# Two blocks on one core: the second block's q, k, v and u weights split earlier, the pooling operand split between rounds of the top-k choice

## The chip, the cores and the metric

The kernel runs on one NeuronCore of a Trainium2 chip. The metric is the device time of one execution in microseconds (us). The kernel is one program in which five engines work side by side, each on its own list of instructions in program order: TensorE (PE), VectorE (DVE), ScalarE (ACT), GpSimd (POOL) and SyncE (SP), which issues the loads. They wait for each other through semaphores only.

## What is computed

256 rows of 1024 channels go through two blocks, all in float32. The change lies in the first half of the second block:

```python
h = rmsnorm_2(x, mix_norm[l])
z = h @ w_in[l]                      # 1024 -> 2632 columns
u = z[..., OFF_POOL:OFF_Q]           # 512, for the pooling mixer
q, k, v = ...                        # 512 columns each, 8 heads of 64
qi, ki, wi = ...                     # index queries 8 x 64, index key 64, index weights 8
q = apply_rope(rmsnorm_2(q, q_norm[l]), cos_a, sin_a)
k = apply_rope(rmsnorm_2(k, k_norm[l]), cos_a, sin_a)
qi = apply_rope(qi, cos_i, sin_i)
ki = apply_rope(rmsnorm_2(ki, idx_k_norm[l])...)
y_pool = pool_mixer(u, pool_w[l], pool_scale[l])      # windowed means, then 4 products of 128 x 128
y_attn = dsa_attention(q, k, v, qi, ki, wi)           # each row attends to its 64 best places
x = x + concat([y_pool, y_attn]) @ w_out[l]
# then memory cross-attention (wq, wo) and a mixture of 32 experts, 2 per row
```

`dsa_attention` scores all places with the index heads (the sum over heads of `relu(qi . ki) * wi`), keeps the 64 best per row, and runs a softmax over them.

## The kernel before

**Exact products.** A float32 weight is split into a high half and a low half of a format that TensorE multiplies fast. ACT writes the high half (`HI`, line 667), DVE writes the low half, weight minus high half (`ring_low`, line 1182), and for the eight names in `POOLED` POOL writes the low half (line 637). The left operand is split likewise into `AH` and `AL`. A product is then three matmuls (lines 1918 to 1920).

**Units.** `split_order()` lists the weights in the order of use; each is cut into units of 1024 columns per partition, which are numbered over all weights in `S`. In the part that matters the order is qi (4 units), kw (index key and weights, 1 unit), q (4), k (4), v (4), u (4), pool0, pool1, attn0, attn1 (2 each), wq, wo. On ACT `hi_to(n)` makes all high halves up to unit n, on DVE `lo_to(n)` all low halves up to n, passing over those of POOL. `HI` has 8 places, so the high half of unit n waits until TensorE is done with unit n - 8 (`s_un`). So the place where `hi_to` and `lo_to` stand in the lists of ACT and DVE says how far the splits run ahead of TensorE, and what stands in front of them.

**TensorE's order.** Strip qi, transposes of x, kw; strip q (after its third unit the memory keys are turned, `s_hdp`); strip k; the index queries and the index key are turned (`turn_heads`, `s_thp` 1 to 3); index scores (`pair_scores`, `s_scp`, line 2369); strip v; strip u, which waits for ACT's scaled copy of k (`s_z` 8); the pooling products (line 2390, `s_plp` 1 and 2); turning of q and k (`s_thp` 4 to 7); the four products with `pool_w` (line 2402, `s_plp` 3 and 4); the attention scores (`head_scores`, line 2412), which wait for all copies of q and k to `QT` and `KT` (`s_th` 8); then strips of the output projection (`strip_half`) between the steps of the softmax: `probabilities` turns exponentials (line 2421), `values` multiplies with v (line 2430), `rows_turned` turns the result (line 2437). A strip has twelve matmuls of 512 columns per unit; a `strip_half` works for one of the two row tiles and has six.

**ACT around it.** `z_out` copies a strip's result from PSUM to `Z`; `head_sums` sums the squares of 16 heads (line 681) and takes the roots (line 958); `heads_out` copies the strip scaled per head (line 966); line 978 is the root for the index key, line 998 the relu of the index scores. All of these and all `hi_to` stand in one list.

**DVE around it.** `head_sums` (index key: line 1492), `head_turned`, `head_cosine`, `head_sum` are the rotary steps (lines 1501, 1508, 1514), `head_recip` the reciprocal of the roots, `index_heads` the weighted sum over index heads, `index_round` one of 8 rounds of the choice of places (each takes the 8 largest per row, lines 1585 and 1589), `index_mask` the mask from them, `low_out` the low half of the pooling result (`AL`, line 1198).

**POOL** begins its 8 units of pool and attn when DVE has finished the rotary step of k (`s_hk` 8).

**SP** issues the loads in the order of use into a ring of 8 buffers, later 21, each load when its buffer's last user is done. The 96 expert weights of 1 MB each fill the ring from 515 us on.

## Time and profile before

| | us |
|---|---|
| median of 3 runs | 808.61 |
| lowest, highest | 799.5, 809.78 |
| profiled execution | 811.39 |
| its span, first to last instruction | 809.4 |
| TensorE busy | 726.8 (90%) |
| VectorE busy | 364.0 (45%) |
| ScalarE busy | 326.7 (40%) |
| GpSimd busy | 60.7 (8%) |

A profile is one execution on the chip. Times in it count from the first instruction. The stretch of the second block that the change touches lies between 426 and 523 us. PEclk is the clock that TensorE was granted, as a share of 2.4 GHz. A row of the timeline has the start, the duration, the engine, the line, the operation with what it writes and reads, how many instructions are merged, and in brackets the idle time before it with what ended it. Matmuls overlap, so that their durations are longer than the distance of their starts.

### The profile page before, as it was taken

How to read it: one execution, taken by the hardware profiler on the slowest of the kernel's cores; microseconds unless marked ns; L12 is line 12 of the kernel's file. 1: busy time of each engine (PE TensorE's matmuls, PEld its weight loads, DVE VectorE, ACT ScalarE, POOL GpSimd, SP SyncE). 2: the span in 40 equal slices, each digit the busy share in tenths (PEclk: the TensorE clock that was granted, in tenths of full speed). 3: DMA queues.
4: the chain of work that ended last, by engine and by line, in shares of the span. 5: the costliest groups of instructions: out<-in, count | busy, mean ns of one | idle time of the engine just before them, and what ended most of it. 6: DMA issues, size and time to landing. Idle time of an engine off the chain costs nothing.

```text
span 809.4 us, 13077 instructions
## 1 busy us (share of the span) xinstructions
PE 726.8 (90%) x5415; PEld 572.2 (71%) x5416; DVE 364.0 (45%) x745; ACT 326.7 (40%) x696; POOL 60.7 (8%) x71
## 2 busy tenths in 40 slices
PE   6697999989999999999999778997989999779785
PEld 4275677877999999999988556886775666345252
DVE  1453998456644566445586576443441111011011
ACT  2234465454533453334474894667331111001001
POOL 5000002000000002000000018072000000000000
PEclk8699899989999999999898999999979999989889
DMA  9997777616777754454463335455789999999994
GB/s 326 399 360 303 269 259 246 235 53 233 247 252 242 248 184 156 158 183 150 153 206 118 104 107 172 145 207 208 278 346 410 419 421 420 420 421 421 419 406 141
DMA packets 71475, 211.44 MB, mean 261 GB/s; under 512 B 7351, under 2 KB 34133, under 8 KB 55542
## 3 DMA queue, kind: packets, MB, share of 16 engines
q1 hardware_dynamic: 70370, 209.91, 69.0%
q0 software_dynamic: 800, 0.63, 0.4%
q8 instruction: 44, 0.72, 0.4%
q14 instruction: 17, 0.14, 0.1%
q10 hardware_dynamic: 244, 0.03, 0.0%
HBM read 209.51 MB, written 1.05 MB: 260 GB/s over the span
## 4 chain that ended last, share of the span: by engine, by line
PE 64%; DMA 11%; DVE 8%; ACT 6%; SPq 5%; issue 4%; ACTq 0%
PE ps L1918 10%; PE ps L1919 9%; PE ps L1920 9%; SPq L431 5%; PE ps L1931 5%; PE ps L1932 4%; PE ps L1933 4%; PE ps L2588 4%; DMA ring<-in_expert_w_up_dram 4%; DMA ring<-in_expert_w_gate_dram 3%; DVE ring_low L1182 3%; DMA ring<-in_ada_w_dram 2%; PE ps L2000 2%; PE ps L2564 2%; PE ps L2638 2%
## 5 line engine op out<-in xcount | busy, mean ns | idle before, releaser
L1182 DVE TENSOR_TENSOR ring_low<-ring,HI 128x1024 fp32r<-128x1024 f32 (+1 forms) x119 | 143.7, 1249 | 57.8 <-ACT HI L667 57.8
L667 ACT ACTIVATE HI<-ring 128x1024 fp32r<-128x1024 f32 (+1 forms) x135 | 133.9, 1056 | 46.9 <-DMA ring<-in_w_in_dram 45.8
L1918 PE MATMUL ps<-AH,HI 128*128 128x256 f32 x320 | 90.1, 282 | 0.3 <-DVE Z L1428 0.3
L1920 PE MATMUL ps<-AH,ring_low 128*128 128x256 f32 x320 | 89.6, 280 | 0.0
L1919 PE MATMUL ps<-AL,HI 128*128 128x256 f32 x320 | 89.4, 280 | 0.0
L1918 PE MATMUL ps<-HI,AH 128*128 128x512 f32 (+1 forms) x176 | 74.0, 421 | 12.1 <-DVE ring_low L1182 10.1
L2588 PE MATMUL ps<-ring,ZM 128*32 128x256 f32 x880 | 70.0, 413 | 15.3 <-DMA ring<-in_expert_w_up_dram 12.4
L1919 PE MATMUL ps<-ring_low,AH 128*128 128x512 f32 (+1 forms) x176 | 70.5, 401 | 0.0
L1920 PE MATMUL ps<-HI,AL 128*128 128x512 f32 (+1 forms) x176 | 69.7, 396 | 0.0
L2588 PEld LDWEIGHTS ps<-ring,ZM 128*32 128x32 f32 x880 | 38.1, 118 | 39.1 <-DMA ring<-in_expert_w_up_dram 15.8
L1918 PEld LDWEIGHTS ps<-AH,HI 128*128 128x128 f32 x320 | 60.1, 188 | 3.1 <-issue 2.5
L1931 PE MATMUL ps<-AH,HI 128*128 128x256 f32 x192 | 57.9, 302 | 3.3 <-DVE AL L1251 1.7
L1919 PEld LDWEIGHTS ps<-AL,HI 128*128 128x128 f32 x320 | 60.2, 188 | 0.0
L1920 PEld LDWEIGHTS ps<-AH,ring_low 128*128 128x128 f32 x320 | 60.1, 188 | 0.0
L1932 PE MATMUL ps<-AL,HI 128*128 128x256 f32 x192 | 55.3, 288 | 0.0
L1933 PE MATMUL ps<-AH,ring_low 128*128 128x256 f32 x192 | 55.0, 286 | 0.0
L637 POOL TENSOR_TENSOR ring_low<-ring,HI 128x1024 fp32r<-128x1024 f32 x16 | 39.7, 2520 | 196.8 <-DVE Z L1514 165.8
L1918 PEld LDWEIGHTS ps<-HI,AH 128*128 128x128 f32 x176 | 35.5, 201 | 26.5 <-DVE ring_low L1182 14.4
L1931 PE MATMUL ps<-AT,HI 128*128 128x256 f32 x176 | 49.3, 280 | 0.0
L1932 PE MATMUL ps<-AT,HI 128*128 128x256 f32 x176 | 49.2, 280 | 0.0
L1933 PE MATMUL ps<-AT,ring_low 128*128 128x256 f32 x176 | 49.2, 279 | 0.0
L1149 ACT ACTIVATE Z<-ps,GS 128x256 f32<-128x256 f32 x8 | 3.8, 474 | 110.2 <-issue 90.8
(382 smaller groups left out, 1310.9 us busy)
## 6 DMA issues: line engine op xcount, KB each, us to landing
ring<-in_expert_w_up_dram SPq DMA_DIRECT2D x28, 1024.0 KB, 25.3
ring<-in_expert_w_gate_dram SPq DMA_DIRECT2D x27, 1024.0 KB, 26.3
ring<-in_ada_w_dram SPq DMA_DIRECT2D x24, 1024.0 KB, 8.4
ring<-in_expert_w_down_dram SPq DMA_DIRECT2D x23, 1024.0 KB, 21.4
ring<-in_w_ffn_in_dram SPq DMA_DIRECT2D x20, 1024.0 KB, 6.2
ring<-in_w_in_dram SPq DMA_DIRECT2D x17, 1024.0 KB, 5.8
ring<-in_w_ffn_out_dram SPq DMA_DIRECT2D x11, 1024.0 KB, 7.3
ring<-in_w_out_dram SPq DMA_DIRECT2D x8, 1024.0 KB, 5.0
```

Source lines behind the costliest of these rows:

```text
L431: sp.dma_start(dst(views[s]), src, allow_slow_non_contiguous=True).then_inc(W.sems[s], 16)
L637: po.tensor_tensor(W.low(name)[:, o:o + w], W.view(name)[:, o:o + w], HI[:, u % UNITS, 0:w].bitcast(F32), ALU.subtract).then_inc(s_lp, 1)
L667: act(HI[:, i % UNITS, 0:w], W.view(name)[:, o:o + w], ACT.Copy).then_inc(s_hi, 1)
L1182: tt(W.low(name)[:, o:o + w], W.view(name)[:, o:o + w], HI[:, i % UNITS, 0:w].bitcast(F32), ALU.subtract).then_inc(s_lo, 1)
L1918: mm(dst, lh, rh, start=start, stop=False)
L1919: mm(dst, lh, rl, start=False, stop=False)
L1920: return mm(dst, ll, rh, start=False, stop=stop)
L1931: mm(dst, lh, rh, start=start, stop=False, skip_group_check=True)
L1932: mm(dst, lh, rl, start=False, stop=False, skip_group_check=True)
L1933: return mm(dst, ll, rh, start=False, stop=stop, skip_group_check=True)
L2000: ins = mm(ps[7 if q < 3 else 3][32 * j:32 * j + 32, :], cr[:, k, :], v[:, 512 * j:512 * j + 512], start=(k == 0), stop=(k == 7))
L2588: ins = mm(ps[UPB][CAP * j:CAP * j + CAP, 256 * h:256 * h + 256], XG[:, k, CAP * j:CAP * j + CAP], W.view(name)[:, 256 * k:256 * k + 256], ...
```

## The change

Nothing is added to or removed from the computation; instructions move in the lists of ACT, DVE and TensorE. On ACT the squares of the index key stand before the splits of k, and the splits of k, v and u each stand one strip further ahead: the high halves of v are made around the scaled copy of q, those of u around the scaled copy of k. On DVE the splits move likewise; the sum of the index key stands before the last split of q; the weighted sum over all index heads is in one piece before the rotary step of k; all rounds of the choice stand behind the last split of u; and the two halves of the pooling operand (`low_out`) stand behind rounds 6 and 7 instead of after all. On TensorE the turning of k comes after the products with `pool_w`, the copies to `KT` on ACT with it, and two half strips of pool0 and pool1 stand one step earlier in the softmax.

```diff
--- before.py
+++ after.py
@@ -940,7 +940,13 @@
                 else:
                     ac.wait_ge(s_un, S.end["kw"])
                 act(Z[:, t, 2560:NZ], ps[(1, 3)[t]][:, 0:NZ - 2560], ACT.Copy, scale=rs[:, t:t + 1]).then_inc(s_z, 1)
-            hi_to(S.first["q0"] + 3)
+            for t in range(NT):
+                ac.wait_ge(s_z, 2 + t + 1)
+                act(scq[t][:, 0:64], Z[:, t, 2560:2624], ACT.Square).then_inc(s_ha, 1)
+            hi_to(S.first["k0"])
+            ac.wait_ge(s_hki, 3)
+            act(st[:, 0:2], st[:, 0:2], ACT.Sqrt).then_inc(s_ha, 1)
+            hi_to(S.first["k0"] + 2)
 
             def head_sums(name, t0, banks, c0, c):
 
@@ -969,19 +975,11 @@
 
             ac.wait_ge(s_hdp, 1)
             act(KM[:, 0:2, :], ps[6][:, :].rearrange("p (h n) -> p h n", h=2), ACT.Copy, scale=C1[:, XQK + 1:XQK + 2]).then_inc(s_hda, 1)
-            hi_to(S.first["q0"] + 4)
-            hi_to(S.first["q0"] + 5)
-            for t in range(NT):
-                ac.wait_ge(s_z, 2 + t + 1)
-                act(scq[t][:, 0:64], Z[:, t, 2560:2624], ACT.Square).then_inc(s_ha, 1)
-            ac.wait_ge(s_hki, 3)
-            act(st[:, 0:2], st[:, 0:2], ACT.Sqrt).then_inc(s_ha, 1)
-            hi_to(S.first["q0"] + 6)
+            hi_to(S.first["k0"] + 3)
             head_sums("q1", "q", (4, 5), 16, 0)
-            hi_to(S.first["k0"] + 3)
+            hi_to(S.first["v0"])
             heads_out((4, 5), 16, 512, 1)
-            for i in range(1, 4):
-                hi_to(S.first["k0"] + i + 3)
+            hi_to(S.first["v0"] + 3)
 
             for pp in range(2):
                 ac.wait_ge(s_thp, pp + 1)
@@ -998,29 +996,31 @@
                         act(RR[t][:, 4 * quad + par:4 * quad + par + 3:2, 0:w],
                             ps[b][:, :].rearrange("p (i n) -> p i n", i=2)[:, :, 0:w], ACT.Relu).then_inc(s_rel, 1)
             head_sums("k1", "k", (0, 1), 32, 16)
-            hi_to(S.first["v0"] + 3)
+            hi_to(S.first["u0"])
             heads_out((0, 1), 32, 1024, 2)
-            for i in range(1, 4):
-                hi_to(S.first["v0"] + i + 3)
+            hi_to(S.first["u0"] + 3)
             z_out("v1", 1536, 512, (2, 3), "v")
-            for i in range(7):
-                hi_to(S.first["u0"] + i + 3)
+            hi_to(S.first["u0"] + 9)
             z_out("u1", 0, 512, (0, 1), "u")
             hi_to(S.first["wq0"] - 1)
 
             for h in range(2):
                 ac.wait_ge(s_plp, h + 1)
                 act(MT[:, 2 * h:2 * h + 2, :], ps[h][:, :].rearrange("p (g n) -> p g n", g=2), ACT.Copy).then_inc(s_pl, 1)
-            for i in range(4):
-                ac.wait_ge(s_thp, 4 + i)
-                dst, pp = (QT, KT)[i // 2], i % 2
-                act(dst[:, 2 * pp:2 * pp + 2, :], ps[4 + i][:, :].rearrange("p (h n) -> p h n", h=2), ACT.Copy).then_inc(s_th, 1)
+
+            def heads_copied(dst, i):
+                for pp in range(2):
+                    ac.wait_ge(s_thp, 4 + 2 * i + pp)
+                    act(dst[:, 2 * pp:2 * pp + 2, :], ps[4 + 2 * i + pp][:, :].rearrange("p (h n) -> p h n", h=2), ACT.Copy).then_inc(s_th, 1)
+
+            heads_copied(QT, 0)
             for kk in range(2):
                 ac.wait_ge(s_plp, 2 + kk + 1)
                 for k in (2 * kk, 2 * kk + 1):
                     ins = act(AH[:, k, :], ps[2 + kk][:, 256 * (k % 2):256 * (k % 2) + 256], ACT.Copy,
                               scale=C2[:, PSC + k:PSC + k + 1])
                 ins.then_inc(s_ah, 1)
+            heads_copied(KT, 1)
             warm(ACT.Exp)
 
             def exponents(t, nh, w, c):
@@ -1522,39 +1522,39 @@
                 for t in range(NT):
                     tt(zz[t], zz[t], bc(hs[:, t, :], 2, [P, nh, 64]), ALU.mult).then_inc(sm, 1)
 
-            lo_to(S.first["q0"] + 3)
+            def head_recip(c0, ca):
+
+                ve.wait_ge(s_ha, ca)
+                ve.reciprocal(st[:, c0:c0 + 16], st[:, c0:c0 + 16]).then_inc(s_kn, 1)
+
             head_turned(2048, 8, rope[:, 0], rope[:, 1], 0, s_hqi)
             head_cosine(2048, 8, rope[:, 0], 4, s_hqi)
-            lo_to(S.first["q0"] + 4)
+            head_sums(2560, 1, s_hki, 0)
+            lo_to(S.first["q0"] + 3)
             head_sum(2048, 8, 4, s_hqi)
-            ve.wait_ge(s_hdp, 2)
-            ts(KM[:, 2:4, :], ps[7][:, :].rearrange("p (h n) -> p h n", h=2), C1[:, XQK + 1:XQK + 2], None, ALU.mult).then_inc(s_hdv, 1)
-            lo_to(S.first["q0"] + 5)
+            lo_to(S.first["k0"])
             ve.wait_ge(s_hqi, 8)
-            head_sums(2560, 1, s_hki, 0)
             ve.wait_ge(s_tab, 9)
             head_turned(2560, 1, CG[:, 2], SN[:, 2], 2, s_hki)
             head_cosine(2560, 1, CG[:, 2], 7, s_hki)
-            lo_to(S.first["q0"] + 6)
+            lo_to(S.first["k0"] + 1)
             head_sum(2560, 1, 7, s_hki)
             head_norm(2560, 1, 11, s_hki, 0)
             for t in range(NT):
                 ts(st2[:, 8 + 8 * t:16 + 8 * t], Z[:, t, 2624:2632], float(64 ** -0.5 * 8 ** -0.5), None,
                    ALU.mult).then_inc(s_wi, 1)
-            def head_recip(c0, ca):
-
-                ve.wait_ge(s_ha, ca)
-                ve.reciprocal(st[:, c0:c0 + 16], st[:, c0:c0 + 16]).then_inc(s_kn, 1)
-
+            lo_to(S.first["k0"] + 2)
+            ve.wait_ge(s_hdp, 2)
+            ts(KM[:, 2:4, :], ps[7][:, :].rearrange("p (h n) -> p h n", h=2), C1[:, XQK + 1:XQK + 2], None, ALU.mult).then_inc(s_hdv, 1)
+            lo_to(S.first["k0"] + 3)
             head_recip(16, 5)
-            lo_to(S.first["k0"] + 3)
+            lo_to(S.first["v0"])
             ve.wait_ge(s_hki, 14)
             head_turned(512, 8, CG[:, 0], SN[:, 0], 4, s_hq)
             head_cosine(512, 8, CG[:, 0], 4, s_hq)
-            lo_to(S.first["k0"] + 4)
+            lo_to(S.first["v0"] + 1)
             head_sum(512, 8, 4, s_hq)
-            lo_to(S.first["k0"] + 5)
-            lo_to(S.first["k0"] + 6)
+            lo_to(S.first["v0"] + 3)
 
 
             def index_heads(h0):
@@ -1595,28 +1595,21 @@
                     ve.wait_ge(s_ix, 48 + t + 1)
                     ts(SX[:, 1, t, 0:w], SX[:, 0, t, 0:w], -2.0e38, -1.0e30, ALU.is_gt, ALU.mult).then_inc(s_ix, 1)
 
-            index_heads(0)
-            index_heads(2)
+            for h in range(0, 8, 2):
+                index_heads(h)
+            index_bound()
             head_recip(32, 7)
-            lo_to(S.first["v0"] + 3)
-            index_heads(4)
-            index_heads(6)
-            index_bound()
-            lo_to(S.first["v0"] + 4)
+            lo_to(S.first["u0"])
             ve.wait_ge(s_hq, 8)
             head_turned(1024, 8, CG[:, 1], SN[:, 1], 6, s_hk)
             head_cosine(1024, 8, CG[:, 1], 4, s_hk)
-            lo_to(S.first["v0"] + 5)
+            lo_to(S.first["u0"] + 1)
             head_sum(1024, 8, 4, s_hk)
-            index_round(0)
-            lo_to(S.first["u0"] + 2)
-            index_round(1)
-            index_round(2)
             lo_to(S.first["u0"] + 3)
-            for i in range(3, 8):
+            for i in range(8):
                 index_round(i)
-            for kk in range(2):
-                low_out(OP_POOL + kk + 1, kk, 2 + kk, C2[:, PSC:PSC + 4])
+                if i > 5:
+                    low_out(OP_POOL + i - 5, i - 6, i - 4, C2[:, PSC:PSC + 4])
 
             def added(t, n, name, b, c):
 
@@ -2394,8 +2387,6 @@
                     ins.then_inc(s_plp, 1)
             te.wait_ge(s_hq, 8)
             turn_heads(512, (4, 5))
-            te.wait_ge(s_hk, 8)
-            turn_heads(1024, (6, 7))
             te.wait_ge(*W.ready("pw"))
             for gi in range(4):
                 te.wait_ge(s_pl, gi // 2 + 1)
@@ -2403,6 +2394,8 @@
                          start=True, stop=True)
                 if gi % 2:
                     ins.then_inc(s_plp, 1)
+            te.wait_ge(s_hk, 8)
+            turn_heads(1024, (6, 7))
 
 
             def head_scores(t, heads, dst):
@@ -2448,15 +2441,15 @@
                 strip_half(0, (f"pool{n}",), SUB[0][n], OP_POOL + 1, 0, stop=False, per=1)
             te.wait_ge(s_asc, 2)
             head_scores(1, range(4, 8), lambda h: ps[ASB[1] + h % 2][:, 256 * (h // 2 - 2):256 * (h // 2 - 2) + 256])
+            strip_half(1, ("pool0",), SUB[1][0], OP_POOL + 2, 0, stop=False)
             te.wait_ge(s_exp, 1)
             te.wait_ge(s_asc, 4)
             for i in range(2):
                 probabilities(0, i, 1, 1 + i)
-            strip_half(1, ("pool0",), SUB[1][0], OP_POOL + 2, 0, stop=False)
+            strip_half(1, ("pool1",), SUB[1][1], OP_POOL + 2, 0, stop=False)
             te.wait_ge(s_pta, 2)
             te.wait_ge(s_asc, 6)
             values(1, 8, 1, v_heads, PTs[0])
-            strip_half(1, ("pool1",), SUB[1][1], OP_POOL + 2, 0, stop=False)
             rows_turned(0, 1)
             te.wait_ge(s_exp, 2)
             for i in range(4):
```

## Rows read from the trace of the kernel before

**Rows 1.** The page: GB/s moved in each of the 40 slices of 20.2 us
```profile
GB/s 326 399 360 303 269 259 246 235 53 233 247 252 242 248 184 156 158 183 150 153 206 118 104 107 172 145 207 208 278 346 410 419 421 420 420 421 421 419 406 141
```

**Rows 2.** Windows: busy us and count per engine, clock, DMA share, GB/s
```profile
449.00:457.00 8.00, 4.09 (x12) 3.17 (x12) 3.39 (x7) 7.87 (x30) 0.00 (x0) 0.80 0.21 81
...
491.00:496.00 5.00, 4.59 (x12) 3.34 (x12) 5.00 (x26) 0.73 (x2) 5.00 (x3) 0.66 0.00 0
```

**Rows 3.** TensorE's waits (us, times, longest); the page's group of DVE's splits
```profile
PE ps L1918 <- DVE ring_low L1182: 10.1, 5, 3.9
...
L1182 DVE TENSOR_TENSOR ring_low<-ring,HI 128x1024 fp32r<-128x1024 f32 (+1 forms) x119 | 143.7, 1249 | 57.8 <-ACT HI L667 57.8
```

**Rows 4.** Timeline of TensorE in the strips q and k
```profile
437.36 0.47 PE L1918 MATMUL ps<-HI,AH 128*128 128x512 f32 x1
...
452.99 0.50 PE L1918 MATMUL ps<-HI,AH 128*128 128x512 f32 x1 [3.91 <-DVE ring_low L1182]
```

**Rows 5.** Timeline of ACT, from the index key's root to k's first square sum
```profile
443.59 0.20 ACT L978 ACTIVATE st<-st 128x2 f32<-128x2 f32 x1 [3.52 <-DVE st L1494]
...
444.65 0.20 ACT L681 ACTIVATE CN<-ps 128x64 f32<-128x64 f32 x1
...
450.64 1.04 ACT L667 ACTIVATE HI<-ring 128x1024 fp32r<-128x1024 f32 x1
451.58 3.37 ACT L966 ACTIVATE Z<-ps,st 128x64 f32<-128x64 f32 x16
454.73 3.06 ACT L667 ACTIVATE HI<-ring 128x1024 fp32r<-128x1024 f32 x3
458.07 1.09 ACT L988 ACTIVATE YT<-ps 128x512 f32<-128x512 f32 x2 [0.28 <-PE ps L2350]
...
464.49 0.25 ACT L681 ACTIVATE CN<-ps 128x64 f32<-128x64 f32 x1
```

**Rows 6.** Timeline of TensorE: first index score, and the start of v
```profile
459.92 1.16 PE L2369 MATMUL ps<-XN,YT 64*128 64x128 f32 x16 [1.00 <-issue]
...
463.31 0.50 PE L1918 MATMUL ps<-HI,AH 128*128 128x512 f32 x1
```

**Rows 7.** Timeline of TensorE in v and u: units behind a wait
```profile
472.88 0.50 PE L1918 MATMUL ps<-HI,AH 128*128 128x512 f32 x1 [1.06 <-DVE ring_low L1182]
...
480.90 0.50 PE L1918 MATMUL ps<-HI,AH 128*128 128x512 f32 x1 [0.76 <-DVE ring_low L1182]
...
491.34 0.79 PE L1918 MATMUL ps<-HI,AH 128*128 128x512 f32 x1 [2.63 <-DVE ring_low L1182]
```

**Rows 8.** Timeline of DVE beside u: the turn of k, two splits
```profile
476.96 1.43 DVE L1501 TENSOR_TENSOR SR<-Z,CN 128x256 f32<-128x256 f32 x4
...
483.15 2.48 DVE L1182 TENSOR_TENSOR ring_low<-ring,HI 128x1024 fp32r<-128x1024 f32 x1
...
487.90 3.38 DVE L1182 TENSOR_TENSOR ring_low<-ring,HI 128x1024 fp32r<-128x1024 f32 x1
```

**Rows 9.** The instructions of POOL's line 637: ns min/median/max
```profile
L637 POOL TENSOR_TENSOR ring_low<-ring,HI x16: 2360/2407/3397, 482.1 to 550.3; 128x1024 fp32r<-128x1024 f32 x16
```

**Rows 10.** Timelines of TensorE, ACT and DVE from pooling to the softmax
```profile
496.75 0.67 PE L2390 MATMUL ps<-ring,Z 128*128 128x256 f32 x2 [0.82 <-issue]
...
501.10 1.11 ACT L1017 ACTIVATE KT<-ps 128x512 f32<-128x512 f32 x2
...
503.01 2.03 PE L2412 MATMUL ps<-KT,QT 64*128 64x128 f32 x24
...
505.31 1.29 DVE L1653 SCALAR_TENSOR_TENSOR SR<-ps,XN 128x512 f32<-128x512 f32 x2
...
510.69 1.13 PE L2412 MATMUL ps<-KT,QT 64*128 64x256 f32 x8
...
515.73 0.51 ACT L1030 ACTIVATE SR<-SR,st 128x256 f32<-128x256 f32 x1 [2.19 <-DVE st L1648]
...
522.61 0.66 PE L2421 MATMUL ps<-ident,SR 128*128 128x128 f32 x4 [0.70 <-DVE PT L1679]
```

## The prediction

> **What bounds the kernel now.** I read the page first, then the windows, then the waits of TensorE, and then the timeline of one stretch engine by engine. The page's row of bytes shows two parts [rows 1]: in the 28 slices up to 567 us the DMA engines move 53 to 399 GB/s and are not the limit, from about 607 us they stand at 406 to 421 GB/s until the last slice. So the last quarter is a stream of expert weights at full rate. Its start is not free, though: each expert load waits for a buffer that a step of the attention stages gives back. If those stages end earlier by some amount, the stream starts and ends earlier by that amount.
>
> In the stretch from 426 to 523 us it is TensorE's own order that counts. Its waits for `ring_low` from L1182 are 10.1 us in five waits [rows 3]. They all sit in the strips k, v and u: 3.91 us in k, 1.06 in v, and three in u, of which 0.76 and 2.63 are shown [rows 4, 7]. After the first and the last of them the granted clock falls: 0.80 from 449 to 457 us, 0.66 from 491 to 496 us [rows 2]. A unit of twelve 512-column matmuls takes 2.8 us otherwise (v's first three: 472.88 - 1.06 - 463.31 = 8.5 us [rows 6, 7]) and 4.6 us from 491.34 to u's end at 496.75 - 0.82 = 495.93 [rows 7, 10]: that is the level of 1.2 GHz for most of it instead of 2.4.
>
> **Why the splits are late.** ACT makes the high half of a weight unit, DVE the low half, both in program order. ACT sat 3.52 us in front of the square root L978, because DVE came late to the key's sum [rows 5]. Then the sixteen square sums of q and their roots ran from 444.65, and only at 450.64 did it make the high half of k's last unit, while TensorE had been dry since 452.99 - 3.91 = 449.1 [rows 4, 5]. In u DVE had rounds of the choice of places in front of the last two splits, and these splits took 2.48 and 3.38 us instead of the usual 1.25 [rows 3, 8].
>
> **The change, part by part.** It adds and removes no instruction; everything moves, so each term is a shift.
>
> *k and the index scores.* The squares and the sum of the index key come before k's splits; ACT no longer waits at L978 and makes k's units from 429 to 433 us, its last right after the copy of KM at 438. The square sums of q can start when q's first half is done: 437.36 + 1.4 + 0.2 = 439.0 (half a unit and a semaphore behind the start of its last unit [rows 4]) instead of 444.65. From there ACT's chain keeps its lengths [rows 5]: sums and roots 5.99 (to 450.64), one split 0.94, scaled copies 3.15, three splits 3.06, and from the copy of the turned heads to TensorE's first score 459.92 - 458.07 = 1.85. Sum: 439.0 + 5.99 + 0.94 + 3.15 + 3.06 + 1.85 = 454.0. TensorE itself would be there a little sooner: k starts at 440.2, four units of 2.8 end at 451.4, and the turned heads need to follow within 0.7. So the stall of 3.91 us and the slow clock behind it go, ACT's copies are what is late next, and the scores start at 454.0 instead of 459.92 [rows 6]: **5.9 us**.
>
> *v and u.* Counted from the first score: v starts 3.39 later (463.31 - 459.92), its four units, all split before the scores, take 11.1 [rows 6, 7]. u waits for the scaled copies of k: ACT begins k's sums 4.57 after the first score (464.49 [rows 5]), plus 5.99, 0.94 and 3.37 gives 14.9; with the semaphore u starts 15.0 after, 0.5 later than TensorE could. u's second unit is split behind the turn and the cosine of k: from DVE's start on them to TensorE's next unit it is 480.90 - 476.96 = 3.94 [rows 7, 8], so 1.1 more than a unit: a new stall. Third and fourth unit come after the sum of k and one split each, 1.25 apiece, in time but for about 0.4. End of u: 15.0 + 3.94 + 3 x 2.8 + 0.1 = 27.4 after the first score; before it was 495.93 - 459.92 = 36.0. That is **8.5 us**, u ending at 481.4.
>
> What covers the rounds of the choice now? Eight of them at 1.2 us (two of them stand between the splits of [rows 8]: 487.90 - 485.63 = 2.3) run to about 486 to 488 us, behind pooling and the turning. The four low halves of pooling stand among them, so DVE is free for the mask at about 490.5, and the mask is wanted at 489.6 plus one us for the scores. That is a near tie; before, DVE was also last (505.31 against scores that start at 503.01 [rows 10]).
>
> *The turning of k put behind the pooling products.* The same matmuls, but the two copies of KT (L1017), which ran behind the products, now come after them: about 1.1 us between the last turn and the first score [rows 10]. Pooling starts 0.82 after u as before, so scores at 481.4 + 0.8 + 6.26 + 1.1 = 489.6 (before 503.01): shift 13.4. **Cost 1.1 us** (between 0, if DVE's mask is last anyway, and 1.5).
>
> *Half a strip put ahead of the turned probabilities.* TensorE was not waiting there; now ACT gets them 2.8 us later and its second exponentials (515.73 - 510.69 = 5.04 after the scores) start about 0.5 later; the first product with v follows both halves of the strip, so the turn of its rows must wait for DVE's scaling (0.7). I take **0.7 us of cost** where the order meets again, at 522.61 [rows 10]; it could be 0 to 1.5.
>
> Sum: 5.9 + 8.5 - 1.1 - 0.7 = **12.6 us**. Behind 522.61 nothing changes and every release of a buffer shifts alike. The span of 809.4 becomes 796.8; the profiled execution took 811.39, so it becomes 798.8. The median of the three runs shown is 808.61, 2.8 below that execution; I forecast **796.0** for the median, 1.6% less.
>
> **Two prices that the trace gives only in part.** POOL's splits begin when the sum of k is done, now at about 474 instead of 482.13, in the midst of DVE's last two splits. The trace shows what that costs: while POOL runs (2.36 to 3.40 us each [rows 9]) DVE's splits of 483.15 and 487.90 took 2.48 and 3.38, so 1.2 and 2.1 too long, and some of POOL's own took 3.4. The rounds between them kept their length. The forecast holds one such collision, hidden but for 0.4. The mask L1596 never ran beside POOL; from below it costs nothing more, from above the 2.1 of a split, twice. The Trainium skill, "SBUF — State Buffer", section "Who interferes with whom", states that a DVE instruction with two SBUF inputs, and a tensor_scalar in a two-port mode, blocks fully against a GpSimd instruction that reads SBUF; the trace agrees for the splits (2.48 and 3.38), and by this rule the mask would wait as well. The rule speaks against this change, since it moves POOL's work onto more of DVE's.
>
> **The rivals.**
> *A: the port eats part.* POOL gets in ahead of both of DVE's splits: u's third unit 1.9 us late, its fourth 0.7, and the mask waits up to 2 x 2.1, of which the strips of pooling on TensorE hide about 2. That gives back 3 to 5: 799 to 801. For it: both late splits in [rows 8]; against it: DVE's next split is issued as the sum ends, before POOL's semaphore arrives. The skill's rule gives this outcome.
> *B: the gain is lost in the stream.* If the DMA engines were already bound before the first shifted release, the end would stay: 808. For it: 346 GB/s already from 587 to 607 us, with loads piled up [rows 1]. Against it: from 506 to 567 us, when the expert loads begin, it is 145 to 208 GB/s, less than half of the full rate, and they are issued on TensorE's and ACT's releases, all of which shift.
> *C: slower.* The clock: TensorE without pauses is granted 1.2 GHz for longer. A unit at that level costs 1.8 more (4.6 against 2.8); seven units turn the gain into nothing, and sixteen make it 2% slower, 825. k, v, u and pooling have about 17. Against it: both falls of [rows 2] come behind pauses of 3.91 and 2.63 us, and none behind those of 1.06 and 0.76 us [rows 4, 7].
> *D: more than the sum.* If the two reorders cost nothing and u's second unit does not stall, it is 12.6 + 1.8 + 1.1 = 15.5, and the shorter pauses leave the clock up once more (1.8): 17.3, 791.
>
> **How the numbers follow.** Forecast (gain 9.5 to 15) 0.62; A 0.17; B 0.06; C 0.03 (over 2% slower 0.02); D 0.12. Without C these cases hold 791 to 808. The three runs of before differ by 10 us (799.5 to 809.78), mostly downward from the median, so the low end goes to 788; B and C left out, the high end is A's 801 with 2 for the runs: 803. Range 788 to 803. About 2% (16 us) is what a measurement can tell from no change. Faster by more: D and the forecast's upper edge, 0.18. Slower by more: 0.02. Within 2%: 0.80.
>
> **What would show it.** In the profile after: TensorE's waits for `ring_low` in k gone, in u one of about 1.1 us before the second unit; no wait of 3.5 us at L978; first index score near 454, u's end near 481.4, first attention score near 489.6, the fourth turn of probabilities near 510.0; the granted clock near 1.0 where it was 0.80 and 0.66; the last quarter the same 420 GB/s, only earlier by 12.6. Wrong would be: POOL's first split before DVE's third of u, a long mask, or the same stream end with an earlier 510.

## The result, and the profile after

| | before | after |
|---|---|---|
| median, us | 808.38 (799.5 to 814.02, 20 runs) | 797.84 (790.06 to 802.48, 20 runs) |
| ratio of the two, 95% interval | | 0.9866 (0.9841 to 0.989) |
| span of the profiled execution, us | 809.4 | 798.3 |

The change makes the kernel 1.3% faster, 10.5 us by the medians. The forecast was 796.0, with a gain of 12.6. The ratio leaves out runs more than 1.5% above the fastest of their kernel, so it is not exactly that of the medians.

The page's GB/s of the kernel after, for the same 40 slices as [rows 1]: the last quarter is the same stream at 420 GB/s, only its end has moved.

```profile
GB/s 320 403 361 286 277 223 272 237 106 92 378 215 213 211 182 218 200 167 133 203 168 150 140 108 218 106 211 210 333 335 425 420 421 420 420 420 421 419 407 147
```

Windows of the kernel after, columns as in [rows 2]. Where the granted clock was 0.80 and 0.66 it is now 1.00, the level of 2.4 GHz.

```profile
449.00:457.00 8.00, 6.70 (x47) 5.47 (x45) 5.87 (x11) 7.12 (x21) 0.00 (x0) 1.00 0.67 231
491.00:496.00 5.00, 4.44 (x35) 3.65 (x36) 5.00 (x8) 1.99 (x4) 5.00 (x3) 1.00 0.98 282
```

TensorE's waits in the kernel after (us, times, longest). Five waits of 10.1 us for DVE's splits [rows 3] have become one of 1.0. The copy of KT is a new wait of 1.0.

```profile
PE ps L2405 <- ACT KT L1014: 1.0, 1, 1.0
PE ps L1911 <- DVE ring_low L1182: 1.0, 1, 1.0
```

TensorE's timeline of the kernel after: start, duration, and in brackets the idle time before it and what ended it. In this order: q's last unit, first index score, start of v, start of u, u's second unit, pooling, first attention scores, the first and the fourth turn of probabilities (L2414).

```profile
439.21 0.47 PE L1911 MATMUL ps<-HI,AH 128*128 128x512 f32 x1
...
455.70 1.16 PE L2362 MATMUL ps<-XN,YT 64*128 64x128 f32 x16 [1.17 <-issue]
...
459.09 0.50 PE L1911 MATMUL ps<-HI,AH 128*128 128x512 f32 x1
...
470.65 0.50 PE L1911 MATMUL ps<-HI,AH 128*128 128x512 f32 x1 [0.29 <-ACT Z L972]
...
474.65 0.50 PE L1911 MATMUL ps<-HI,AH 128*128 128x512 f32 x1 [0.97 <-DVE ring_low L1182]
...
484.20 0.67 PE L2383 MATMUL ps<-ring,Z 128*128 128x256 f32 x2 [0.82 <-issue]
...
491.56 2.03 PE L2405 MATMUL ps<-KT,QT 64*128 64x128 f32 x24 [1.03 <-ACT KT L1014]
...
503.14 1.03 PE L2414 MATMUL ps<-ident,SR 128*128 128x128 f32 x8
...
512.11 0.66 PE L2414 MATMUL ps<-ident,SR 128*128 128x128 f32 x4 [0.70 <-DVE PT L1672]
```

ACT of the kernel after. The wait of 3.52 us at the key's root [rows 5] is one of 0.67 and lies nine microseconds earlier. The split behind the sums (446.88), the copies of q and the three splits keep their lengths. The last line is the first exponential of the softmax.

```profile
434.29 0.20 ACT L948 ACTIVATE st<-st 128x2 f32<-128x2 f32 x1 [0.67 <-DVE st L1494]
...
446.88 1.04 ACT L667 ACTIVATE HI<-ring 128x1024 fp32r<-128x1024 f32 x1
447.83 3.35 ACT L972 ACTIVATE Z<-ps,st 128x64 f32<-128x64 f32 x16
450.97 3.06 ACT L667 ACTIVATE HI<-ring 128x1024 fp32r<-128x1024 f32 x3
...
499.75 0.40 ACT L1030 ACTIVATE SR<-SR,st 128x128 f32<-128x128 f32 x1 [6.72 <-DVE st L1641]
```

DVE and POOL of the kernel after: DVE's last two splits of u, the mask L1596, the first tile's masked scores and negated maxima, and POOL's splits, which end at 496.58 and so run beside the first two of these rows.

```profile
475.72 4.58 DVE L1182 TENSOR_TENSOR ring_low<-ring,HI 128x1024 fp32r<-128x1024 f32 x2
...
492.45 4.42 DVE L1596 TENSOR_SCALAR XN<-XN 128x128 f32<-128x128 f32 x2
...
496.96 1.29 DVE L1646 SCALAR_TENSOR_TENSOR SR<-ps,XN 128x512 f32<-128x512 f32 x2
...
499.54 0.17 DVE L1641 TENSOR_SCALAR st<-st 128x8 f32<-128x8 f32 x1
```

```profile
475.88 20.70 POOL L637 TENSOR_TENSOR ring_low<-ring,HI 128x1024 fp32r<-128x1024 f32 x8 [154.49 <-DVE Z L1514]
```

The mask ran beside POOL and took 4.42 us. In the kernel before POOL had ended its splits at 502.85, and the same two instructions took 0.42:

```profile
504.79 0.42 DVE L1596 TENSOR_SCALAR XN<-XN 128x128 f32<-128x128 f32 x2
```

**How kernels are compared below.** From one profile to another, the stretch up to q's last unit ends between 435.48 and 442.10 us, and the stretch from the fourth turn of probabilities to the end lasts 282.3 to 289.1, also where the code of these stretches is the same. So each kernel is measured by three distances on TensorE that repeat within about 0.1 us where the code is the same (D2 of e6 is the one exception, 0.2 less, see there): **D1** from q's last unit to the first index score, **D2** from there to the first pooling product, **D3** from there to the fourth turn of probabilities.

| kernel | D1 | D2 | D3 (of it to the first attention score) | sum | median, us (runs) |
|---|---|---|---|---|---|
| before | 22.56 | 36.83 | 25.86 (6.26) | 85.25 | 808.38 (20) |
| after | 16.49 | 28.50 | 27.91 (7.36) | 72.90 | 797.84 (20) |
| e1 key only | 18.08 | 34.56 | 27.24 (6.26) | 79.88 | 805.03 (10) |
| e2 splits only | 16.49 | 28.53 | 31.09 (6.26) | 76.11 | 802.27 (10) |
| e3 half strips back | 16.48 | 28.52 | 31.24 (7.36) | 76.24 | 803.8 (1) |
| e4 turn of k back | 16.45 | 28.51 | 27.69 (6.26) | 72.65 | 799.69 (1) |
| e5 mask free | 16.48 | 28.49 | 27.94 (7.37) | 72.91 | 799.12 (1) |
| e6 mask free, half strips back | 16.51 | 28.32 | 27.64 (7.36) | 72.47 | 799.77 (1) |
| e7 k's last split late | 18.04 | 29.91 | 27.95 (7.36) | 75.90 | 803.79 (1) |
| e8 u's second split early, POOL held | 16.50 | 27.61 | 27.92 (7.36) | 72.03 | 794.61 (1) |
| e9 best | 16.45 | 27.58 | 26.52 (6.26) | 70.55 | 793.94 (6) |
| e10 after again, beside e9 | 16.48 | 28.51 | 27.96 (7.36) | 72.95 | 797.59 (6) |
| e11 mask and negated maxima free, half strips back | 16.48 | 28.52 | 26.94 (7.36) | 71.94 | 792.44 (1) |
| e12 best, POOL held longer | 16.48 | 27.59 | 26.53 (6.26) | 70.60 | 793.99 (6) |

The change's own account by distances: D1 6.07 less, D2 8.33 less, D3 2.05 more, together 12.35 us.

### The profile page after: what moved, and what is told of

The parts are those of the page before. It is cut to its first block, busy times and chain, and to the rows that moved or that the text cites. A ratio compares the mean times of both kernels' runs of the same rounds, so it can differ in the third digit from the quotient of the medians.

```text
span 798.3 us, 13076 instructions
## 1 busy us (share of the span) xinstructions
PE 724.5 (91%) x5415; PEld 573.3 (72%) x5416; DVE 366.5 (46%) x745; ACT 326.4 (41%) x696; POOL 60.8 (8%) x71
## 4 chain that ended last, share of the span: by engine, by line
PE 66%; DMA 12%; DVE 7%; ACT 5%; SPq 5%; issue 4%; ACTq 0%; DVEq 0%
PE ps L1911 10%; PE ps L1912 10%; PE ps L1913 9%; SPq L431 5%; PE ps L1924 5%; PE ps L1925 5%; PE ps L1926 5%; PE ps L2581 4%; DMA ring<-in_expert_w_up_dram 4%; DMA ring<-in_expert_w_gate_dram 3%; DMA ring<-in_ada_w_dram 2%; PE ps L1993 2%; PE ps L2557 2%; DVE ring_low L1182 2%; PE ps L2631 2%
## 5 line engine op out<-in xcount | busy, mean ns | idle before, releaser
L1911 PE MATMUL ps<-HI,AH 128*128 128x512 f32 (+1 forms) x176 | 71.5, 407 | 2.0 <-DVE ring_low L1182 1.0
L1912 PE MATMUL ps<-ring_low,AH 128*128 128x512 f32 (+1 forms) x176 | 68.8, 391 | 0.0
L1911 PEld LDWEIGHTS ps<-AH,HI 128*128 128x128 f32 x320 | 60.1, 188 | 3.1 <-issue 2.5
L1924 PEld LDWEIGHTS ps<-AH,HI 128*128 128x128 f32 x192 | 38.7, 202 | 10.3 <-issue 6.4
```

The lines of the kernel that those rows point to most:

```text
L1911: mm(dst, lh, rh, start=start, stop=False)
L1912: mm(dst, lh, rl, start=False, stop=False)
L1924: mm(dst, lh, rh, start=start, stop=False, skip_group_check=True)
```

## The experiments

### The parts of the change

**e1, the key alone.** Built on the kernel before: only the squares, the sum and the root of the index key move. The lines that go at their old places are left out here.

```diff
 on ACT:
+            for t in range(NT):
+                ac.wait_ge(s_z, 2 + t + 1)
+                act(scq[t][:, 0:64], Z[:, t, 2560:2624], ACT.Square).then_inc(s_ha, 1)
             hi_to(S.first["q0"] + 3)
+            ac.wait_ge(s_hki, 3)
+            act(st[:, 0:2], st[:, 0:2], ACT.Sqrt).then_inc(s_ha, 1)
 on DVE:
-            lo_to(S.first["q0"] + 3)
             head_turned(2048, 8, rope[:, 0], rope[:, 1], 0, s_hqi)
             head_cosine(2048, 8, rope[:, 0], 4, s_hqi)
+            head_sums(2560, 1, s_hki, 0)
+            lo_to(S.first["q0"] + 3)
```

> The kernel before with one part of the change alone: the squares, the sum and the root of the index key come early on ACT and DVE; every split stays where it was. Three distances on TensorE are compared, since the stretch ahead of them varies from run to run: D1 from q's last unit to the first index score (22.6 us before, 16.5 after), D2 from there to the first pooling product (36.8 before, 28.5 after), D3 from there to the fourth turn of probabilities of the second tile (25.9 before, 27.9 after). Theory (ACT's 3.5 us in front of the root of the key was the cause in k): the square sums of q start 4 us earlier, the wait in k before its last unit falls from 3.9 us to under 0.5, D1 is 18.4, D2 and D3 stay; 4 us less in all. Rival (the place of the splits is the cause): the last split of k still stands behind the sums, the wait stays above 2.5 us, D1 above 21.

D1 fell to 18.08, 4.48 of the 6.07 that the whole change brings there. The time was 0.996 of the one before (0.993 to 0.999). Timelines of e1, of ACT, TensorE, DVE and TensorE again: the root of the key, the first and second index scores, two splits of u, the mask, the first turn of probabilities. The last line is a window on the second index scores.

```profile
431.19 0.20 ACT L948 ACTIVATE st<-st 128x2 f32<-128x2 f32 x1 [1.62 <-DVE st L1494]
...
455.86 1.16 PE L2369 MATMUL ps<-XN,YT 64*128 64x128 f32 x16 [2.12 <-issue]
457.33 3.56 PE L2369 MATMUL ps<-XN,YT 64*128 64x256 f32 x16 [0.30 <-ACT SR L998]
...
480.54 2.47 DVE L1182 TENSOR_TENSOR ring_low<-ring,HI 128x1024 fp32r<-128x1024 f32 x1
...
485.28 1.21 DVE L1182 TENSOR_TENSOR ring_low<-ring,HI 128x1024 fp32r<-128x1024 f32 x1
...
498.46 2.25 DVE L1596 TENSOR_SCALAR XN<-XN 128x128 f32<-128x128 f32 x2
...
506.83 1.09 PE L2421 MATMUL ps<-ident,SR 128*128 128x128 f32 x8 [1.34 <-ACT SR L1030]
```

```profile
457.00:461.00 4.00, 3.70 (x18) 2.54 (x18) 2.04 (x3) 1.99 (x6) 0.00 (x0) 0.57 0.02 6
```

The root no longer stands in front of q's sums, and TensorE no longer waits in k, so the wait of ACT was the cause in k. The rest of the 6.07 is e7's place, below. D2 and D3 were expected to stay, and both moved. D2 fell by 2.27, the sum of a gain and a loss. DVE's last split of u now fell between two of POOL's and took 1.21 instead of 3.38 [rows 8]; TensorE waited 0.43 there instead of 2.63, with no slow clock behind it, and the two together are 3.7 less. Against that, TensorE paused 2.12 ahead of the first index scores; behind the pause the granted clock was 0.57, and the second scores took 3.56 instead of 2.00. D3 rose by 1.38, because the mask fell beside POOL (2.25) and TensorE then waited 1.34 for the exponentials behind it.

**e2, the splits alone.** The changed kernel, with the turn of k and both half strips back in their old places (the edits of e3 and e4 together; ACT's copies and the second half strip, shown there, go with them).

```diff
             turn_heads(512, (4, 5))
+            te.wait_ge(s_hk, 8)
+            turn_heads(1024, (6, 7))
             te.wait_ge(*W.ready("pw"))
 in the softmax:
-            strip_half(1, ("pool0",), SUB[1][0], OP_POOL + 2, 0, stop=False)
             te.wait_ge(s_exp, 1)
             te.wait_ge(s_asc, 4)
             for i in range(2):
                 probabilities(0, i, 1, 1 + i)
+            strip_half(1, ("pool0",), SUB[1][0], OP_POOL + 2, 0, stop=False)
```

> The changed kernel with both of TensorE's reorders taken back (the turn of k and its copies, the two half strips); the order of the splits and of the rounds stays as changed. D1 16.5 and D2 28.5 as in the changed kernel. Theory P (the mask blocks against POOL on the shared port, and the half strip covers that): the mask still ends with POOL's last split, the first attention score comes 1.1 us earlier, but TensorE then waits about 4 us for the first exponentials in front of the turn of probabilities: D3 about 29.7, the kernel about 1.8 us slower than the changed one. Rival (the reorders cost 1.8 us, as the prediction's sum has it, and the mask does not matter): D3 25.9, the kernel 2 us faster than the changed one.

D1 and D2 are those of the whole change, 16.49 and 28.53: all of its gain is in the order of splits and sums. D3 is 31.09, 3.2 longer than with the two reorders, and 1.4 longer than expected: the slow clock behind a pause of 3.54 was not in that sum. The time was 0.9889 (0.9849 to 0.9929), the median 802.27.

**e3, the half strips back.**

```diff
             te.wait_ge(s_asc, 2)
             head_scores(1, range(4, 8), ...)
-            strip_half(1, ("pool0",), SUB[1][0], OP_POOL + 2, 0, stop=False)
             te.wait_ge(s_exp, 1)
             te.wait_ge(s_asc, 4)
             for i in range(2):
                 probabilities(0, i, 1, 1 + i)
-            strip_half(1, ("pool1",), SUB[1][1], OP_POOL + 2, 0, stop=False)
+            strip_half(1, ("pool0",), SUB[1][0], OP_POOL + 2, 0, stop=False)
             te.wait_ge(s_pta, 2)
             te.wait_ge(s_asc, 6)
             values(1, 8, 1, v_heads, PTs[0])
+            strip_half(1, ("pool1",), SUB[1][1], OP_POOL + 2, 0, stop=False)
```

> The changed kernel with only the two half strips back in their old places. Theory P: TensorE waits about 2.8 us for the first exponentials, D3 about 29.7. Rival (no cover needed): D3 27.2, 0.7 less than the changed kernel.

TensorE's timeline at the first turn of probabilities, and the window behind it:

```profile
505.38 1.09 PE L2414 MATMUL ps<-ident,SR 128*128 128x128 f32 x8 [2.60 <-ACT SR L1030]
```

```profile
505.00:511.00 6.00, 5.62 (x24) 4.66 (x25) 2.09 (x3) 5.25 (x20) 0.00 (x0) 0.72 0.00 0
```

With the half strip back, TensorE stands 2.60 us, and in the stretch behind that pause the granted clock is 0.72 where it is 1.00 without. D3 is 31.24. Against 26.94, the same order with no wait (e11, below), that is 4.3: 2.6 of waiting and 1.7 of slower matmuls. So the moved half strip, costed as a loss of 0.7, is a cover: it costs 0.97 (27.91 against 26.94) and takes 4.3 away. The wait was expected at about 2.8, the slow clock was not expected.

**e4, the turn of k back.**

```diff
             turn_heads(512, (4, 5))
+            te.wait_ge(s_hk, 8)
+            turn_heads(1024, (6, 7))
             te.wait_ge(*W.ready("pw"))
             ...
-            te.wait_ge(s_hk, 8)
-            turn_heads(1024, (6, 7))
 on ACT:
             heads_copied(QT, 0)
+            heads_copied(KT, 1)
             for kk in range(2):
             ...
-            heads_copied(KT, 1)
             warm(ACT.Exp)
```

> The changed kernel with only the turn of k and the copies to KT back in their old places. The first attention score comes 1.1 us earlier after the first pooling product (6.3 instead of 7.4). Theory P: the first exponentials are bound by the mask and so by POOL's last split, TensorE loses the 1.1 us again in front of the turn of probabilities, D3 27.9 as in the changed kernel. Rival (the 1.1 us is a plain cost): D3 26.8.

The first scores come 1.10 earlier, as costed, but D3 is only 0.22 shorter: the mask still ended last, and TensorE waited 0.60 for the exponentials.

### POOL and the mask

**e5, the mask free of POOL.** POOL starts its splits of `attn1` only when the mask is made.

```diff
 on POOL, ahead of the wait for the high half:
+                    if name == "attn1" and o == 0:
+                        po.wait_ge(s_ix, 52)
```

> The changed kernel; POOL waits with its last two splits (attn1) until DVE has written the mask, so nothing of POOL runs beside the mask. Theory P (shared port): the two mask instructions take 0.45 us together instead of 4.4, the first exponentials end 4 us earlier, and nothing on TensorE changes, since the half strip hid it: D3 27.9. Rival (the mask is long for another reason, such as waiting for rounds of the choice): it stays above 3 us.

Timeline of DVE in e5, the mask and the first negated maxima (128x8):

```profile
494.92 0.42 DVE L1598 TENSOR_SCALAR XN<-XN 128x128 f32<-128x128 f32 x2
...
498.02 2.18 DVE L1643 TENSOR_SCALAR st<-st 128x8 f32<-128x8 f32 x1
```

The mask took its 0.42, 4.0 less, but D3 stayed at 27.94. Half of what was freed went to the next small instruction, which now fell beside POOL (2.18 instead of 0.17). The other 2.0 reach ACT's exponentials, and there nobody waits for them: in the changed kernel they end at 502.9, and TensorE is in the moved half strip until 503.14. The mask's 4 us are hidden, by a margin of 0.2.

**e6, the mask free and the half strips back.** The edits of e3 and e5 together.

```diff
+                    if name == "attn1" and o == 0:
+                        po.wait_ge(s_ix, 52)
 in the softmax:
-            strip_half(1, ("pool0",), SUB[1][0], OP_POOL + 2, 0, stop=False)
             te.wait_ge(s_exp, 1)
             ...
+            strip_half(1, ("pool0",), SUB[1][0], OP_POOL + 2, 0, stop=False)
```

> The same, and the two half strips back in their old places (the third kernel of the first set without the port). Theory P: no wait of TensorE for the first exponentials, D3 26.9, 4.3 less than with the half strips back and the port busy (31.2), and 1.0 less than the changed kernel: the half strips cost 0.7 to 1.0 when there is nothing to cover. Rival (the half strips' place costs 3 us by itself): D3 stays near 31.

DVE and TensorE in e6: mask, negated maxima, first turn of probabilities.

```profile
489.99 0.43 DVE L1598 TENSOR_SCALAR XN<-XN 128x128 f32<-128x128 f32 x2
...
493.10 2.18 DVE L1643 TENSOR_SCALAR st<-st 128x8 f32<-128x8 f32 x1
```

```profile
498.56 1.09 PE L2416 MATMUL ps<-ident,SR 128*128 128x128 f32 x8 [0.63 <-ACT SR L1032]
```

D3 is 27.64 instead of the 26.9 that were expected with no wait: the negated maxima again, and 0.63 of TensorE's waiting behind them. Against e3 it is 3.6 less, so the mask beside POOL is what made e3's pause. D2 is 28.32 here, 0.2 less than in the kernels with the same code there: DVE's last two splits of u took 2.35 together, and POOL's first took 4.46 instead of 2.4. In the others the two take turns: POOL's first and second take 3.3 and 3.4, and DVE's pair 4.57 to 4.59.

**e11, the negated maxima free too.** The edit of e3, and POOL waits for the negated maxima of the first tile in place of the mask.

```diff
+                    if name == "attn1" and o == 0:
+                        po.wait_ge(s_mxs, 2)
```

> The sixth kernel (half strips back, nothing of POOL beside the mask), with POOL's last two splits held until the negated maxima of the first tile are written as well. There that instruction of 128 x 8 took 2.18 us instead of 0.17 and TensorE waited 0.63 for the first exponentials. Theory P: it takes 0.2 us, the wait goes, D3 falls from 27.6 to 26.9. Rival (its length had another cause): D3 stays at 27.6.

The same rows in e11:

```profile
491.82 0.17 DVE L1643 TENSOR_SCALAR st<-st 128x8 f32<-128x8 f32 x1
```

```profile
496.57 1.09 PE L2416 MATMUL ps<-ident,SR 128*128 128x128 f32 x8
```

Nothing waits, and D3 is 26.94: 7.36 to the first score and 19.58 behind it, where the kernel before has 6.26 and 19.60. So D3's added 2.05 of the change is 1.10 for the copies of KT and 0.95 for the half strip.

### The splits of k and u

**e7, k's last split late again.** Tests whether this one place made the pause in k: its high half goes back behind q's square sums, all else stays.

```diff
-            hi_to(S.first["k0"] + 3)
             head_sums("q1", "q", (4, 5), 16, 0)
+            hi_to(S.first["k0"] + 3)
             hi_to(S.first["v0"])
```

> The changed kernel with k's last high half back behind the square sums of q, where it stood before. Theory (ACT's list as a chain sets the first index score): the chain is one split shorter ahead of the sums but one longer behind them, TensorE does not wait in k (under 0.4 us), and the first index score comes 0.0 to 1.0 us later: D1 16.5 to 17.5. Rival (running a strip ahead is what took the wait of 3.9 us away): the wait in k comes back with more than 2 us and the slow clock behind it, D1 above 20.

TensorE in e7, first and second index scores, and a window on the second:

```profile
455.08 1.16 PE L2362 MATMUL ps<-XN,YT 64*128 64x128 f32 x16 [2.76 <-issue]
456.55 3.50 PE L2362 MATMUL ps<-XN,YT 64*128 64x256 f32 x16 [0.30 <-ACT SR L996]
```

```profile
457.00:461.00 4.00, 4.00 (x20) 2.80 (x17) 1.26 (x2) 2.05 (x5) 0.00 (x0) 0.59 0.02 4
```

TensorE waits for no low half in k here either: with the sums early, the split behind them is still in time. But D1 is 18.04, 1.55 longer, above the 16.5 to 17.5 that were expected and nearly that of e1 (18.08), where the split stands at the same place: two high halves now stand between the sums and the scaled copies (1.0), and DVE's reciprocal, which stands behind the low half of the late unit, kept ACT 0.50 more. TensorE, done with k as before, paused 2.76 us ahead of the scores; behind that the granted clock was 0.59, the second scores took 3.50 instead of 2.00, and D2 grew by 1.4. So with the key's root out of the way, ACT's chain from the sums to the scaled copies and the splits behind them sets the scores, and TensorE's own wait for a split does not.

**e8, u's second split before the turn of k, POOL held.**

```diff
 on DVE:
-            lo_to(S.first["u0"])
+            lo_to(S.first["u0"] + 1)
             ve.wait_ge(s_hq, 8)
             head_turned(1024, 8, CG[:, 1], SN[:, 1], 6, s_hk)
             head_cosine(1024, 8, CG[:, 1], 4, s_hk)
-            lo_to(S.first["u0"] + 1)
+            lo_to(S.first["u0"] + 2)
 on POOL, once, ahead of its splits:
+            po.wait_ge(s_lo, S.number[S.first["u0"] + 3])
```

> The changed kernel with two edits around u: DVE makes the low half of u's second unit before the turn of k instead of behind it (and the third before the sum of k), and POOL starts only when DVE is done with u's splits. Theory: the wait of 0.97 us before u's second unit goes and DVE's last two splits of u take 1.2 us each instead of 4.6 together; D2 falls from 28.5 to 27.4. POOL's splits lie about 3 us later, so they still meet the mask: D3 27.5 to 29.5. Rival (u is bound by the scaled copies alone): D2 stays at 28.5.

DVE in e8, u's last split and the mask:

```profile
475.47 1.22 DVE L1183 TENSOR_TENSOR ring_low<-ring,HI 128x1024 fp32r<-128x1024 f32 x1
...
489.28 4.09 DVE L1597 TENSOR_SCALAR XN<-XN 128x128 f32<-128x128 f32 x2
```

The wait of 0.97 before u's second unit is gone (one of 0.24 before the third is left), D2 is 27.61, 0.9 less, and the last split has its 1.22. D3 is unchanged: the mask merely meets POOL later.

### A faster version, and what bounds it

**e9** takes the splits of the change, e8's two edits, both reorders undone, and POOL held ahead of `attn0` until the first tile's negated maxima. **e10** is the changed kernel again, on the same chip. **e12** is e9 with POOL held once more for the second tile's maxima. Ahead of POOL's splits, the first three lines are in e9 too:

```diff
+            po.wait_ge(s_lo, S.number[S.first["u0"] + 3])
+                    if name == "attn0" and o == 0:
+                        po.wait_ge(s_mxs, 2)
+                    if name == "attn1" and o == 0:
+                        po.wait_ge(s_mxs, 4)
```

> A version built from what the first eight runs showed: the splits and the rounds as in the changed kernel; u's second low half ahead of the turn of k; both of TensorE's reorders back in their old places; POOL starts after DVE's last split of u and stops after pool0 and pool1 until DVE has written the mask and the negated maxima of the first tile, so that no tensor_scalar of DVE meets it. Theory (the port is the only thing that the half strips covered, and the later copies of KT are a plain cost once the port is free): D1 16.5, D2 27.6, D3 25.9, 70.0 together against 72.9 in the changed kernel: 2.9 us faster than the changed kernel. Rival (the low halves of pooling come too late behind the earlier scores): a wait for AL before the first strips of pool0, D3 above 27, at most 1.5 us faster.

> The changed kernel itself, on the same chip as the version before this one, for the ratio between them, and to see how far the three distances repeat: D1 16.5, D2 28.5, D3 27.9 each within 0.1, while the time up to q's last unit may differ by several us (436.9 to 442.1 so far).

> The ninth kernel with one wait more: POOL makes attn0's two low halves behind the first tile's negated maxima, and attn1's two behind the second tile's. In the ninth kernel that second instruction of 128 x 8 took 0.84 us instead of 0.17 beside POOL's last split, and D3 was 26.5 instead of the 25.9 expected. Theory P: it takes 0.17, D3 is 25.9, the three distances sum to 69.9, 15.3 less than before and 3.0 less than the changed kernel; the ratio to the kernel before is 0.979 to 0.983. Rival: attn1's low half comes too late for its strip, a new wait of TensorE for ring_low behind the softmax eats it.

The times against the kernel before: e9 0.9809 (0.9769 to 0.9849), e12 0.9825 (0.9778 to 0.9872), e10 0.9876 (0.9828 to 0.9925). The distances of e9 are 2.4 shorter than those of the changed kernel; the medians of e9 and e10 are 3.65 apart (six runs each, 792.1 to 795.3 and 794.9 to 804.3), and the intervals of their ratios overlap.

D3 of e9 is 26.52, not 25.86. I had put the rest on the second tile's negated maxima (0.84 in e9). e12 brought them to 0.17, and D3 stayed at 26.53: that theory falls. TensorE in e12 shows what is left:

```profile
496.60 1.09 PE L2419 MATMUL ps<-ident,SR 128*128 128x128 f32 x8 [0.61 <-ACT SR L1035]
```

With the turn of k ahead of the products with `pool_w`, these start 0.9 later (4.44 us after the first pooling product in e12, 3.56 in e11), and so do ACT's high halves, DVE's low halves, the mask and the masking of the first tile's scores, which starts 9.64 after the first pooling product in e12 and 8.77 in e11. TensorE has its scores 1.1 earlier and then waits 0.61 for the exponentials. Of the 1.1 us that the copies of KT cost, 0.4 is had back in this way (26.94 to 26.53). I hadn't seen that the same reorder also brings the pooled operand forward.

But TensorE and ACT had this same order in the kernel before, where D3 is 25.86 and TensorE did not wait. What differs is DVE's list. Here are the low halves of the pooling operand and the mask, first in e12, then the low halves in the kernel before:

```profile
487.31 0.88 DVE L1203 SCALAR_TENSOR_TENSOR AL<-ps,C,AH 128x256 fp32r<-128x256 f32 x2 [2.49 <-ACT AH L1026]
...
489.27 0.87 DVE L1203 SCALAR_TENSOR_TENSOR AL<-ps,C,AH 128x256 fp32r<-128x256 f32 x2
490.05 0.42 DVE L1601 TENSOR_SCALAR XN<-XN 128x128 f32<-128x128 f32 x2
```

```profile
503.13 1.74 DVE L1198 SCALAR_TENSOR_TENSOR AL<-ps,C,AH 128x256 fp32r<-128x256 f32 x4 [5.98 <-ACT AH L1021]
```

Both start 6.38 after the first pooling product. In e12 the last round of the choice stands between the two halves, a part of the change, and DVE stands idle for 2.49 ahead of them. So the mask starts 9.12 after the first pooling product, and 8.04 in the kernel before. That is 1.08 later, and TensorE waits 0.61 of it. No run moves that round back ahead of the low halves; by these rows it would remove the 0.61 (an estimate).

## Why the prediction was right, step by step

- **k and the index scores, 5.9.** Measured 6.07. From q's last unit to the first score 16.64 were forecast, 16.49 measured, with the chain as named: sums, one split, scaled copies, three splits (446.88 to 453.81 in the ACT rows). e1 shows the root of the key as the cause of the pause and of 4.5 of the gain, and e7 shows ACT's chain as what is late next and the place of k's last split as the other 1.5. The forecast of the first score, 454.0, came out as 455.70, since q's last unit itself began 1.85 later in this profile.
- **v and u, 8.5.** Measured 8.33. u starts 14.95 after the first score (15.0 forecast), its second unit 18.95 (18.94), its stall is 0.97 (1.1), its end 27.68 (27.4: 484.20 - 0.82 - 455.70). POOL's first split began at 475.88, in the midst of DVE's last two, and cost them 2.2 (4.58 instead of 2.35), but D2 only 0.2 (e6). The waits named are gone and the one new wait is as forecast; no run separates the parts of the reorder here (splits a strip ahead, the weighted sum in one piece, the rounds behind the last split).
- **The turn of k, -1.1.** Measured 1.10 to the scores; but only 0.4 to the end of D3 (e12 against e11), because the reorder also starts DVE's chain 0.9 earlier, which the step left out; the round between the low halves of the pooling operand has a part in this. The lower end named, 0 if DVE's mask is last anyway, is what e4 shows (0.22).
- **The half strips, -0.7.** Measured 0.97 (the kernel after against e11), but the step's premise, that TensorE was not waiting there, is right only for the kernel before. With the splits in their new order the mask falls beside POOL and the place has a wait of 2.6, with a slower clock behind it; the half strip covers both. The size was nearly right because two effects that the sum left out, the mask's 4.0 more and its cover, cancel. That is luck: the prediction named a long mask as a sign of being wrong, it came, and it cost nothing only because the half strip stood where it did.
- **The sum, 12.6.** Measured 12.35 in the distances. The span fell by 11.1: 12.35, less 1.85 in front of q's last unit, plus 0.60 behind the fourth turn. The medians fell by 10.5. What takes the remaining 1.8 between 12.35 and 10.5 is open. Outside the three distances instructions have moved only beside strip q, which takes 10.55 up to its last unit before and 10.71 after. The strip of kw, in front of it, already starts 3.49 later in the profile after. The other stretches have the same code and vary from profile to profile by more than 1.8. The two executions shown differ there in the granted clock, as in this window of both kernels, before first (0.87), after second (0.83):

```profile
140.00:180.00 40.00, 36.79 (x257) 33.24 (x258) 19.34 (x34) 20.37 (x34) 0.00 (x0) 0.87 0.44 158
```

```profile
140.00:180.00 40.00, 34.90 (x228) 31.47 (x228) 20.95 (x39) 21.14 (x35) 0.00 (x0) 0.83 0.49 168
```

  e10, the same code, has a span of 793.2 against 798.3, and distances that agree with it within 0.05. So a single profile's span can't settle 1.8 us.
- **The two prices the trace gave in part.** The collision came in both places. The rows of after show the split pair 2.2 longer and the mask 4.0 longer (up to 2 x 2.1 was named). "SBUF — State Buffer", section "Who interferes with whom", in the Trainium skill says a tensor_scalar that enters a two-port mode contends with GpSimd and the later of the two blocks fully; e5 and e6 agree even for one of 128x8 (2.18 instead of 0.17). The scores from PSUM (1.29) and the rounds of the choice kept their lengths beside POOL (e5, where POOL's last two splits run from 495.43 to 500.18, and the kernel after); the first agrees with the same section, where a DVE instruction with one SBUF input outside those modes does not contend.
- **Rival A, the port eats part (799 to 801).** Its mechanism is there, its price is not: of the mask's 4.0 nothing reaches D3, for the strips and the moved half strip hide it. It needed u's third unit 1.9 late, and that unit was on time. Without the moved half strips its price is there too: the distances of e2 and e3 sum to 3.2 and 3.3 more than those of the kernel after, within the 3 to 5 that it named.
- **Rival B, lost in the stream.** Excluded: the stream is the same 420 GB/s, and from the fourth turn to the end it is 286.8 us before and 286.2 after.
- **Rival C, the clock.** No fall in 440 to 512 of the kernel after. In this stretch of all profiles falls stood only behind pauses of 2.12 (e1), 2.60 (e3), 2.63 and 3.91 [rows 4, 7], 2.76 (e7) and 3.54 us (e2), and none behind 0.97 (after), 1.34 (e1) or 1.76 (before, in u). But ahead of it the clock also falls with no pause: here in strip q of the kernel after, behind 5.4 us of matmuls of 72 columns without a gap. The kernel before has a fall that ends at 429.5, e11 has none in this strip. So the rival's mechanism exists, though the change did not bring it.

```profile
429.00:433.00 4.00, 4.00 (x12) 3.09 (x12) 3.83 (x10) 3.88 (x9) 0.00 (x0) 0.57 0.78 263
```

- **Rival D, more than the sum (791).** Not reached by the change: u's second unit stalls, and both reorders cost. e8, e9 and e12 remove the stall and get 793 to 795.

## What to carry to other kernels

A split, or any preparation, is late because of what stands ahead of it in its engine's list, so cost a reorder by writing down each engine's chain from the last thing it truly waits for; done so, the gains in the first two distances came out within 0.2 us. Where the reorder moves one engine's work beside another that shares a port, find the longest instruction that may now block and ask what TensorE has to do in that time: in e3 against the kernel after, work placed in that gap was worth the pause and the slower clock behind it. Compare such changes by distances between two instructions inside the kernel; here they repeat within 0.2 us, while spans of the same code differ by 5.

## What the runs showed of the hardware

- DVE's small tensor_scalar of 128x8, 0.17 us by itself, took 2.18 beside POOL's subtraction of 2.4 us (e5, e6). The two of the mask, 0.42 together, took from 2.25 to 4.42, by where they fell in POOL's row of splits: 4.42 when they began 16.6 us after the row (after), 3.41 at 17.5 (e4), 2.25 at 18.9 (e1).
- How long each of the two engines waits is not settled by the code. In nine profiles with the same code at the end of u, POOL starts beside DVE's last two splits; in eight the two take turns and DVE's pair takes 4.57 to 4.59, in one (e6) it takes its 2.35 and POOL's first split 4.46.
- A pause of TensorE can cost twice. The window of 6 us around the end of a pause of 2.60 has a granted clock of 0.72, and the slow matmuls cost 1.7 more (e3); behind 2.76 it is 0.59 over 4 us and costs 1.4 (e7), behind 2.12 it is 0.57 and costs 1.6 (e1). Behind 1.76 (before) it stayed at 1.00.
